# Experts' combination as two fp32r products over a full array instead of four float32 column tiles

## The reference, cut to what matters

```
def moe_swiglu(h, w_router, w_gate, w_up, w_down):
    ...
    top_val, top_idx = lax.top_k(logits, TOP_K)
    gates = jax.nn.softmax(top_val, axis=-1)
    ...
    def expert_block(args):
        xb, e = args
        return swiglu(xb, w_gate[e], w_up[e], w_down[e])
    out = lax.map(expert_block, (buf.reshape(n_blocks, MOE_BLOCK, D), block_expert)).reshape(P, D)
    contrib = out[dest] * gate_sorted[:, None].astype(out.dtype)
    y = jnp.zeros((T, D), h.dtype).at[tok_sorted].add(contrib)
    return y.reshape(B, S, D)
```

## Time and profile before

| | us |
|---|---|
| median of 3 runs | 1496.59 (1494.72 to 1496.73) |
| the profiled execution | 1494.55 |
| its span, first to last instruction | 1492.8 |
| PE busy | 1384.7 (93%) |
| DVE busy | 645.8 (43%) |
| ACT busy | 286.9 (19%) |
| POOL busy | 127.3 (9%) |

### The profile page before, as it was taken

One profiled execution on the slowest core, in us unless ns is written; L12 is line 12 of the kernel. 1 busy time (PEld: TensorE's weight loads), 2 busy tenths in 40 slices (PEclk: granted clock), 3 DMA queues, 4 the chain that ended last, 5 costly groups with the idle time before them and its releaser, 6 DMA issues.

```text
span 1492.8 us, 27468 instructions
## 1 busy us (share of the span) xinstructions
PE 1384.7 (93%) x11688; PEld 757.2 (51%) x11688; DVE 645.8 (43%) x1421; ACT 286.9 (19%) x407; POOL 127.3 (9%) x106
## 2 busy tenths in 40 slices
PE   5877899999967779999999999999999999999995
PEld 4644788888857754555553333333333333334441
DVE  4545544444579632423423433334324424433433
ACT  3555234434335300001001001001001001001000
POOL 6400111111136200000000000000000000000000
PEclk9889999999978879999999999999999999999998
DMA  9311355455630569997999999999999999999980
GB/s 346 125 56 44 139 177 190 169 196 197 201 117 8 192 236 319 395 391 289 392 393 379 394 393 370 396 393 370 393 394 370 393 395 368 393 396 370 393 341 29
DMA packets 183704, 429.17 MB, mean 287 GB/s; under 512 B 6814, under 2 KB 17104, under 8 KB 183344
## 3 DMA queue, kind: packets, MB, share of 16 engines
q1 hardware_dynamic: 182544, 424.57, 77.0%
q0 software_dynamic: 1056, 3.02, 0.6%
HBM read 426.51 MB, written 1.05 MB: 286 GB/s over the span
## 4 chain that ended last, share of the span: by engine, by line
PE 87%; DVE 9%; issue 2%; ACT 1%; DMA 1%; POOL 0%; DVEq 0%; SPq 0%; POOLq 0%; ACTq 0%
PE psum L1110 62%; PE psum L354 7%; PE psum L355 7%; PE psum L356 7%; DVE x_br L1502 1%; DVE res L1365 1%; DMA raw<-in_mla_w_in 1%; ACT w_hi L331 1%; PE psum L948 1%; PE psum L937 1%; PE psum L928 1%; PE psum L927 0%; DVE xn_lru L1487 0%; DVE xn_lru L1525 0%; DVE xn_lru L1273 0%
## 5 line engine op out<-in xcount | busy, mean ns | idle before, releaser
L1110 PE MATMUL psum<-raw_more,hT 128*32 128x512 f32 x1920 | 615.5, 592 | 0.0
L1110 PE MATMUL psum<-raw_more,xg 128*32 128x512 f32 x2688 | 399.4, 592 | 0.0
L1110 PE MATMUL psum<-raw,xg 128*32 128x512 f32 x2688 | 391.5, 592 | 1.0 <-DVE xg L1606 1.0
L1110 PE MATMUL psum<-raw,hT 128*32 128x512 f32 x768 | 252.1, 592 | 0.0
L1110 PEld LDWEIGHTS psum<-raw,xg 128*32 128x32 f32 x2688 | 124.1, 110 | 213.9 <-issue 204.1
L1110 PEld LDWEIGHTS psum<-raw_more,xg 128*32 128x32 f32 x2688 | 129.9, 110 | 200.3 <-issue 184.0
L1625 DVE STREAM_TRANSPOSE hT<-hid 32x128 f32<-32x128 f32 x672 | 202.9, 302 | 10.3
L1110 PEld LDWEIGHTS psum<-raw_more,hT 128*32 128x32 f32 x1920 | 165.6, 110 | 80.8 <-issue 72.5
L816 ACT ACTIVATE hid<-psum 96x512 f32<-96x512 f32 x56 | 33.2, 593 | 705.5 <-PE psum L1110 705.5
L1617 DVE SCALAR_TENSOR_TENSOR hid<-hid,psum 96x512 f32<-96x512 f32 x56 | 38.2, 682 | 252.2 <-PE psum L1110 252.2
L331 ACT ACTIVATE w_hi<-raw 128x2048 fp32r<-128x2048 f32 (+3 forms) x67 | 123.7, 1883 | 30.9 <-PE psum L356 22.0
(11 more groups left out here) (255 smaller groups left out, 1343.5 us busy)
## 6 DMA issues: line engine op xcount, KB each, us to landing
raw_more<-in_moe_w_down SPq DMA_DIRECT2D x80, 1024.0 KB, 14.1
raw<-in_moe_w_gate SPq DMA_DIRECT2D x64, 1024.0 KB, 14.4
raw_more<-in_moe_w_up SPq DMA_DIRECT2D x64, 1024.0 KB, 14.5
raw<-in_moe_w_up SPq DMA_DIRECT2D x48, 1024.0 KB, 14.8
raw_more<-in_moe_w_gate SPq DMA_DIRECT2D x48, 1024.0 KB, 15.4
raw<-in_moe_w_down SPq DMA_DIRECT2D x32, 1024.0 KB, 10.2
raw<-in_ffn_w_gate SPq DMA_DIRECT2D x14, 1024.0 KB, 5.1
raw<-in_ffn_w_up SPq DMA_DIRECT2D x14, 1024.0 KB, 5.2
```

Of the source, the lines that this page charges most:

```text
L1110: return pe.matmul(psum[rows_q, bank, cols], stationary, moving, start=start, stop=stop, tile_position=(0, rows_q.start), skip_group_check ...
```

## The change

`onehot_T` gets a copy in fp32r, `onehot_Tr`. It holds zeros and ones. `y_sum` is written as `y_hi` (fp32r, copied by ACT) and `y_lo` (fp32r, `y_sum - y_hi`, by DVE). `combine` is now two products over the full array of 128 columns, `onehot_Tr` with `y_hi` and with `y_lo`, accumulated in PSUM. PE waits for `y_lo_m` in the place of `y_ready_m` and `ohT_ready`. Three buffers are added.

```diff
+            y_hi = sb(s, "y_hi", [SLOT_TOKENS, D], F32R)
+            y_lo = sb(s, "y_lo", [SLOT_TOKENS, D], F32R)
...
+            onehot_Tr = sb(s, "onehot_Tr", [SLOT_TOKENS, T], F32R)
...
+            def y_high(n):
+                act.wait_ge(ohT_ready, n + 1)
+                copy(onehot_Tr[:], onehot_T[:])
+                for d in range(2):
+                    act.wait_ge(y_ready_m, n * 2 + (d + 1))
+                    copy(y_hi[:, d * BANK:(d + 1) * BANK], y_sum[:, d * BANK:(d + 1) * BANK]).then_inc(y_hi_m, 1)
...
                     tanh(n, j)
+                    if j == 1 and not first:
+                        y_high(n - 1)
...
                 main_copies(p * E + (E - 1), range(6))
+                y_high(p * E + (E - 1))
...
                 t, d = i // 2, i % 2
-                for rows_q in QUARTERS:
-                    c0 = t * P + rows_q.start
-                    mm = tile(rows_q, BANK_T[1], slice(0, BANK), onehot_T[:, c0:c0 + 32], y_sum[:, d * BANK:(d + 1) * BANK],
-                              start=True, stop=True)
-                mm.then_inc(comb_ps, 1)
+                tok, cols = slice(t * P, (t + 1) * P), slice(d * BANK, (d + 1) * BANK)
+                pe.matmul(psum[:, BANK_T[1]], onehot_Tr[:, tok], y_hi[:, cols], start=True, stop=False)
+                pe.matmul(psum[:, BANK_T[1]], onehot_Tr[:, tok], y_lo[:, cols], start=False, stop=True
+                          ).then_inc(comb_ps, 1)
...
                             if r == 0:
-                                pe.wait_ge(y_ready_m, n * 2)
-                                pe.wait_ge(ohT_ready, n)
+                                pe.wait_ge(y_lo_m, n * 2)
...
-                pe.wait_ge(y_ready_m, n * 2 + 2)
-                pe.wait_ge(ohT_ready, n + 1)
+                pe.wait_ge(y_lo_m, n * 2 + 2)
...
+            def y_low(n):
+                for d in range(2):
+                    cols = slice(d * BANK, (d + 1) * BANK)
+                    dve.wait_ge(y_hi_m, n * 2 + (d + 1))
+                    dve.tensor_tensor(y_lo[:, cols], y_sum[:, cols], y_hi[:, cols].bitcast(F32),
+                                      ALU.subtract).then_inc(y_lo_m, 1)
...
                     silu(n * STEPS + j)
+                    if j == 1 and not first:
+                        y_low(n - 1)
...
                 sums(p * E + (E - 1))
+                y_low(p * E + (E - 1))
```

More of the change, by code:

```diff
@@ L275, in trunk @@
         y_ready_m = sem("y_ready_m")
+        y_hi_m = sem("y_hi_m")
+        y_lo_m = sem("y_lo_m")
         comb_ps = sem("comb_ps")
```

## The result

| | before | after |
|---|---|---|
| median, us (lowest to highest; runs) | 1495.65 (1494.18 to 1496.73; 4) | 1513.15 (1511.91 to 1514.08; 4) |
| profiled execution, us (its span) | 1494.55 (1492.8) | 1512.27 (1510.5) |
| experts' stage: first gate product to last main product (starts) | 553.87 to 1471.93: 918.1 | 553.32 to 1488.62: 935.3 |
| from there to the end of the span | 20.9 | 21.9 |

The changed kernel is slower, ratio 1.0117 (95%: 1.01 to 1.0135). The forecast was 1495.2 with a range up to 1499.5, so it was wrong, in sign and by 18 us. (The forecast started from a median of 1496.59 before; one run more made it 1495.65.) Of the 17.7 us by which the spans differ, 17.2 lie inside the experts' stage, the stretch in which PE was busy without a gap, and 1.0 behind it; the stage also began 0.5 earlier, before any operation that the change touches.

What follows compares the result with a forecast made beforehand. PE, busy without a gap in the experts' stage, was taken as the bound. Loop turns -2.0 us and last combination +0.65 gave -1.35, so 1496.59 became 1495.2 us, range 1491.0 to 1499.5.

Steps and rivals of the forecast that it cites:

- What bounds the kernel: Experts' stage: PE sets the pace, busy 910.00 of 910.00 us; whatever it gains or loses moves the end one for one.
- PE stays busy throughout: Sign that the forecast is right: PE has no pause while a turn of `combine` costs 0.79 us in the loop.
- the weight transfers: Experts' stage: weights arrive ahead of PE; SP's queue waits 239.7 us for ring units, so a small gain fits.
- the splits: Making `y_hi` and `y_lo` in step 1 of looped experts: costs nothing, with 3.8 us of cover on VectorE.
- the sum: Whole kernel: -2.0 us for the loop's turns and +0.65 for the last combination, -1.35 us in all.
- The products and the switch: 28 looped turns of `combine`: 0.79 us each against 0.86, with 0.095 per array switch; -2.0 us.
- The rivals of a cheap and of a dear switch: Looped turns: cheap, 0.57 us, or 0.70 at half the drain, chance 0.17; dear, 0.92 us and slower, chance 0.13.
- ScalarE and VectorE in the loop: Looped experts: `y_lo` ends about 803.2 us, before PE's first turn at 808.02; no cost.
- The last combination: Behind the last expert: chain +1.4 us, shorter turns -1.0 and -0.25, half clock +0.5; +0.65 us in all.
- The end eats the gain: Rival: loop gains 2.0 us, all end turns at half clock cost 1.6; 1496.2 us, no change; chance 0.12.

Runs made afterwards that it cites:

- the first experiment: Changed kernel with only the head of PE's expert loop moved to slot 108 of its 256-instruction block (`head_slot` 108): 1494.02 us, ratio to before 0.9987.

## Why the prediction was wrong

**What bounds the kernel.** Right as far as it went: PE set the pace. But "PE stays busy throughout", which I took from the earlier trace rows and carried over to the changed kernel, was the failing step: PE stood for 13.0 us at five back edges and 1.0 us once more behind the loop, and half clock behind three of the edges cost 5.1 us. A row that says 910.00 of 910.00 shows that nothing is late; it doesn't show by how much. I asked that question for the weight transfers (239.7 us of slack) and for the splits (3.8 us), and never for the instruction fetches, which had next to none: a branch of 2.2 us under a cover of 2.1. No term of the sum and no rival stood for it. I counted the instructions that the change takes out as work saved and not as code that moves.

**The products and the switch.** Right. The timeline of PE for a turn of the changed kernel:

```profile
809.73 2.31 PE L1125 MATMUL psum<-raw_more,hT 128*32 128x512 f32 x17
811.97 0.50 PE L1144 MATMUL psum<-y_hi,onehot_Tr 96*128 96x512 f32 x1
812.31 0.39 PE L1145 MATMUL psum<-y_lo,onehot_Tr 96*128 96x512 f32 x1
812.63 0.63 PE L1125 MATMUL psum<-raw_more,xg 128*32 128x512 f32 x3
...
813.09 0.60 PE L1125 MATMUL psum<-raw_more,xg 128*32 128x512 f32 x3
```

From the last round's pass to `y_hi` are 0.54 us, to `y_lo` 0.34, to the next round 0.32, in all 1.20; without a turn it would be 0.43, so the next round starts 0.77 later. Its first pass then takes 0.45 in the place of 0.43. From the pass ahead of a turn to the passes behind it, all 28 turns in the loop and the last expert cost 0.80 us, for 0.86 before: a gain of 0.06 for the 0.07 predicted. (The 0.087 in the expectation of the first experiment leaves out the longer pass.) By the parts: into the whole array 0.11 (I took 0.095), products 0.34 apart as from the earlier trace rows, back 0.32 - 0.23 = 0.09 (0.095), and the pass behind it 0.02 longer (0.03). Tiles of 32 columns switch like those of 64 in the earlier trace rows. 28 turns give 1.8 us for the predicted 2.0. The rivals of a cheap and of a dear switch both fall, at 0.57 or 0.70 and at 0.92 us a turn. For each switch 0.09 to 0.11 us was measured; the estimate of 0.053 us, worked out from the figure in the Trainium skill's "TensorE: Matmul & The Clock Gate", "Step-by-step: what each phase is for", is too low for it.

**ScalarE and VectorE in the loop.** Right. In the third expert the last `y_lo` ended at 806.30 and PE's turn began at 811.97. The timeline of both engines:

```profile
804.36 1.14 ACT L617 ACTIVATE y_hi<-y_sum 96x512 fp32r<-96x512 f32 x2
...
805.01 1.29 DVE L1664 TENSOR_TENSOR y_lo<-y_sum,y_hi 96x512 fp32r<-96x512 f32 x2
```

A copy of 512 columns takes 0.617 us at the median (I took 0.63 between the ends of the earlier trace rows), a subtraction 0.684 (0.68). No wait for `y_lo` shows on PE in the loop.

**The last combination.** Right in its parts, a little low. Timeline after:

```profile
1489.95 1.28 DVE L1657 TENSOR_TENSOR y_sum<-y_main,psum 96x512 f32<-96x512 f32 x2 [8.22 <-ACT y_main L617]
1490.67 1.23 ACT L617 ACTIVATE y_hi<-y_sum 96x512 fp32r<-96x512 f32 x2 [0.40 <-DVE y_sum L1657]
1491.33 1.29 DVE L1664 TENSOR_TENSOR y_lo<-y_sum,y_hi 96x512 fp32r<-96x512 f32 x2
1492.68 0.50 PE L1144 MATMUL psum<-y_hi,onehot_Tr 96*128 96x512 f32 x1 [3.47 <-DVE y_lo L1664]
1493.45 0.75 DVE L1671 SCALAR_TENSOR_TENSOR res<-psum,gates,res 128x512 f32<-128x512 f32 x1 [0.83 <-PE psum L1145]
...
1494.26 0.79 PE L1144 MATMUL psum<-y_hi,onehot_Tr 96*128 96x512 f32 x1 [0.84 <-DVE res L1671]
1495.51 0.75 DVE L1671 SCALAR_TENSOR_TENSOR res<-psum,gates,res 128x512 f32<-128x512 f32 x1 [1.31 <-PE psum L1145]
```

From the last main product to the first of the combination: 4.06 us, against 2.68 before, +1.38 (predicted +1.4). The first turn takes 0.77 from PE to DVE (0.81), the other three 1.25 each (1494.26 to 1495.51), at half clock (0.50 granted from 1494.5 to 1500.5); I had charged two, 1.29 each, and given the third 0.48 us less. So +1.0 us in the place of +0.65. "The end eats the gain" had 1.6 for all turns at half clock; three of the four were. In the slot-108 kernel, where nothing else is disturbed, it is this that leaves only part of the 1.8 us.

**The sum without the fetches.** Turns -1.8 and end +1.0 give -0.8 us, against the -1.35 of the sum; the difference is nearly all at the end. The kernel at slot 108 bears it out: 1494.02 against a forecast of 1495.2 for the same operations, inside the range. In its profiled execution the way from the first gate product to the end of the span is 1.4 us shorter than before, of which 0.6 are neither turns nor end and not placed. The miss is one missing term: 5 x 2.6 of pause, 5.1 of half clock behind it, and 1.0 behind the loop's end. It could have been had from the trace of before: branches of 2.2 us in PE's sequencer, 48 instructions less ahead of each, 2.5 us less between the block's edge and the branch. What it could not show is that B would keep its place, since no row of before has the branch anywhere else.

## What to carry over

Where a loop's body is thousands of instructions long, as this one's, its length and place modulo 256 can be part of the schedule: a change that removes instructions from it can cost more than it saves, and must be timed at two or three placements of the loop's head before it is judged. Ahead of a forecast, read the length of the branch and the starts of the instruction fetches as one reads any other transfer: how much later may they come before the engine stands. And of a float32 product that copies values through a one-hot matrix, bf16 parts in the tile form of its neighbours (0.22 us a pass, 0.65 for three) beat two fp32r products that need the array reshaped twice (0.80).

## What the runs showed of the hardware that I had not expected

- With the hint, the backward branch of PE at the end of this loop takes 8.8 us less the time since it entered its block, and never less than about 0.45: from 4.7 us at 4.1 to 0.5 us at 8.4. Some 2.1 us of it are covered by what PE has queued.
- Without the hint it takes 6.2 to 6.4 us at either place tried, and PE stands for some 4.2 us of it.
- With the loop's head 48 slots ahead of its block's end PE lost 1.6 to 1.8 us, about 5 us after the start of a branch that itself was quick (one run).
- Pauses of 2.6 us were followed by about four passes' time at half clock (1.7 us) behind three of five edges, in two kernels alike; pauses of 0.9 us by none; those of some 4.2 us by half clock behind every edge, from three passes to seven. What decides it in the middle case stays open.
- A bf16 pass of four column tiles over 512 columns takes 0.215 to 0.220 us, half of the 0.43 of one of the two passes of a float32 product.
